# State-space layer: tokens to chunks and back as full 128x128 transposes of two groups or two token residues, copied out in strided pieces

## The reference

```
ug = u.reshape(bsz, L, 64, 16)
bu_re = einsum('blgh,gph->blgp', ug, bb_re)          # and bu_im
_, _, s_re, s_im = associative_scan(_ssm_combine, (a_re, a_im, bu_re, bu_im), axis=1)
y = einsum('blgp,ghp->blgh', s_re, c_re) - einsum('blgp,ghp->blgh', s_im, c_im)
y = gelu(y.reshape(bsz, L, 1024) + d_skip * u)
return y * sigmoid(y @ w_glu + b_glu)
```

## Time and profile before

| | us |
|---|---|
| median of 3 runs (lowest, highest) | 1896.31 (1896.26, 1896.64) |
| span of the profiled execution | 1895.6 |
| busy: PE, PEld, DVE | 1865.6, 1516.1, 1251.5 |
| busy: ACT, POOL | 904.5, 470.6 |

### The profile page before, as it was taken

One profiled execution on the slowest core, in us unless ns is written; L12 is line 12 of the kernel. 1 busy time (PEld: TensorE's weight loads), 2 busy tenths in 40 slices (PEclk: granted clock), 3 DMA queues, 4 the chain that ended last, 5 costly groups with the idle time before them and its releaser, 6 DMA issues.

```text
span 1895.6 us, 26223 instructions
## 1 busy us (share of the span) xinstructions
PE 1865.6 (98%) x10196; PEld 1516.1 (80%) x10196; DVE 1251.5 (66%) x1925; ACT 904.5 (48%) x1563; POOL 470.6 (25%) x506
## 2 busy tenths in 40 slices
PE   9999999999999999999999999999999999999998
PEld 7787877888667888968889887888787877688877
DVE  7998785647659436456457855678658467649364
ACT  5546877312288213542233344447545465545333
POOL 0491110574358514015123620020001300000000
PEclk9999999999999999999999999999999999999999
DMA  4226542335222535535626943521123411023221
GB/s 172 92 96 201 162 144 81 111 125 182 94 89 89 167 111 162 185 99 166 193 97 173 219 110 107 136 68 57 57 89 109 152 47 43 34 89 145 93 75 67
DMA packets 70874, 222.16 MB, mean 117 GB/s; under 512 B 17104, under 2 KB 17792, under 8 KB 69728
## 3 DMA queue, kind: packets, MB, share of 16 engines
q1 hardware_dynamic: 43056, 157.83, 25.1%
q0 software_dynamic: 24240, 55.79, 10.6%
q10 hardware_dynamic: 3456, 6.87, 1.3%
HBM read 203.23 MB, written 14.81 MB: 115 GB/s over the span
## 4 chain that ended last, share of the span: by engine, by line
PE 85%; DVE 9%; ACT 3%; issue 1%; DMA 1%; DVEq 0%; POOL 0%; SPq 0%; ACTq 0%
PE bank L489 24%; PE bank L491 23%; PE bank L490 23%; DVE ring_low L451 2%; PE bank L3706 1%; PE bank L2153 1%; PE bank L3739 1%; PE bank L1077 1%; PE bank L2160 1%; PE bank L2353 1%; PE bank L2326 1%; DVE lru_x L2254 1%; DVE sq L706 1%; PE bank L3478 1%; ACT ring_high L446 1%
## 5 line engine op out<-in xcount | busy, mean ns | idle before, releaser
L451 DVE TENSOR_TENSOR ring_low<-ring,ring_high 128x1024 fp32r<-128x1024 f32 x283 | 391.1, 1393 | 260.4 <-ACT ring_high L446 259.9
L446 ACT ACTIVATE ring_high<-ring 128x1024 fp32r<-128x1024 f32 x283 | 297.0, 1056 | 518.9 <-PE bank L491 518.4
L489 PE MATMUL bank<-h_high,ring_high 128*128 128x512 f32 (+1 forms) x1276 | 502.3, 394 | 8.1 <-DVE ring_low L451 6.1
L491 PE MATMUL bank<-h_high,ring_low 128*128 128x512 f32 (+1 forms) x1276 | 490.2, 384 | 0.0
L490 PE MATMUL bank<-h_low,ring_high 128*128 128x512 f32 (+1 forms) x1276 | 489.8, 384 | 0.0
L489 PEld LDWEIGHTS bank<-h_high,ring_high 128*128 128x128 f32 x1276 | 240.2, 188 | 71.6 <-issue 19.2
L490 PEld LDWEIGHTS bank<-h_low,ring_high 128*128 128x128 f32 x1276 | 240.3, 188 | 48.5 <-issue 3.1
L491 PEld LDWEIGHTS bank<-h_high,ring_low 128*128 128x128 f32 x1276 | 240.1, 188 | 48.0
L489 PE MATMUL bank<-gated_high,ring_high 128*128 128x512 f32 (+1 forms) x240 | 85.4, 356 | 1.1 <-DVE gated_low L3308 1.1
L491 PE MATMUL bank<-gated_high,ring_low 128*128 128x512 f32 (+1 forms) x240 | 83.2, 347 | 0.0
L490 PE MATMUL bank<-gated_low,ring_high 128*128 128x512 f32 (+1 forms) x240 | 83.2, 347 | 0.0
(11 more groups left out here) (573 smaller groups left out, 3748.3 us busy)
## 6 DMA issues: line engine op xcount, KB each, us to landing
ring<-slabs SPq DMA_DIRECT2D x289, 512.0 KB, 3.2
acs_rows<-acs_rows POOLq DMA_DIRECT2D x16, 512.0 KB, 4.7
s_outputs<-s_ca POOLq DMA_DIRECT2D x4, 1152.0 KB, 5.0
x<-xT SPq DMA_DIRECT2D x2, 2048.0 KB, 8.6
exp_acs<-acs_rows POOLq DMA_DIRECT2D x16, 256.0 KB, 10.3
s_b<-s_br POOLq DMA_DIRECT2D x8, 512.0 KB, 4.5
s_rows<-s_powers POOLq DMA_DIRECT2D x16, 256.0 KB, 7.4
s_inputs<-s_w POOLq DMA_DIRECT2D x8, 512.0 KB, 3.1
```

The lines of the kernel that those rows point to most:

```text
L446: act.activation(self.ring_high[:, self.splits_before[s] % AHEAD, :], self.ring[:, s % RING, :], ACT.Copy)\
L451: dve.tensor_tensor(self.ring_low[:, s % RING, :], self.ring[:, s % RING, :], self.ring_high[:, self.splits_before[s] % AHEAD, :].bitcast( ...
L489: pe.matmul(out, w[0], x[0], start=start, stop=False, **flags)
L491: return pe.matmul(out, w[1], x[0], start=False, stop=stop, **flags)
```

## The change

`transpose_in` now takes two groups at once: the 128x128 block of `u_tok` for groups 2q and 2q+1 is the weight, the whole identity is the moving operand, and the call is `pe.transpose`. A bank then holds, for each q, group parity on the partition halves and even and odd tokens in alternate columns. ACT sorts this out with four copies per bank in place of one: 64 partitions, 4 by 64 elements, read from PSUM with a step of two elements, written in runs of 64. `transpose_out` takes two token residues at once in the same way; the bank holds the residue's parity on the partition halves and the channel half in the column, and ACT again makes four copies of 64 partitions by 4 by 64 elements, this time with contiguous reads and with writes that step by 8 tokens.

```diff
@@ transpose_in
-                for g in range(8):
-                    w = L.UT[:, 8 * i + g].rearrange("p t h -> p (t h)")
-                    for e in range(2):
-                        t = pe.matmul(C.bank[u.b][half(1 - e), g * NC:g * NC + NC], w, C.ident[:, e:P:2], start=True, stop=True)
+                for q in range(4):
+                    two = L.UT[:, 8 * i + 2 * q:8 * i + 2 * q + 2].rearrange("p g t h -> p (g t h)")
+                    t = pe.transpose(C.bank[u.b][:, q * P:(q + 1) * P], two, C.ident[:])
                 t.then_inc(C.bank_full[u.b], 1)
@@ transpose_out
-                for r in range(8):
-                    for x in range(2):
-                        t = pe.matmul(C.bank[u.b][half(x), r * NC:r * NC + NC], L.YT[b % 2][:, r].rearrange("p k o -> p (k o)"),
-                                      C.ident[:, half(x)], start=True, stop=True)
+                for q in range(4):
+                    two = L.YT[b % 2][:, 2 * q:2 * q + 2].rearrange("p r k o -> p (r k o)")
+                    t = pe.transpose(C.bank[u.b][:, q * P:(q + 1) * P], two, C.ident[:])
                 t.then_inc(C.bank_full[u.b], 1)
@@ evac_u
-                act.activation(L.U[:, 8 * i:8 * i + 8, :].rearrange("p g c -> p (g c)"), C.bank[u.b][:], ACT.Copy)\
-                    .then_inc(C.bank_read[u.b], 1)
+                for n in range(2):
+                    got = C.bank[u.b][half(n), :].rearrange("p (q c e) -> p e q c", q=4, e=2)
+                    for e in range(2):
+                        ins = act.activation(L.U[half(1 - e), 8 * i + n:8 * i + 8:2, :], got[:, e], ACT.Copy)
+                ins.then_inc(C.bank_read[u.b], 1)
@@ back, on ACT
-                    act.activation(y.rearrange("p (c r) -> p r c", r=8), C.bank[u.b][:].rearrange("p (r c) -> p r c", r=8),
-                                   ACT.Copy).then_inc(y_made.sem, 1)
+                    for n in range(2):
+                        got = C.bank[u.b][half(n), :].rearrange("p (q x c) -> p x q c", q=4, x=2)
+                        for x in range(2):
+                            ins = act.activation(L.Y[half(x), i, :].rearrange("p (c q n) -> p n q c", q=4, n=2)[:, n], got[:, x], ACT.Copy)
+                    ins.then_inc(y_made.sem, 1)
```

## The result

The changed kernel takes 1903.67 us (median of 6 runs, 1901.22 to 1906.79), the kernel before 1896.85 us in the same session (6 runs, 1896.26 to 1897.69). The ratio is 1.0035, 95% interval 1.0025 to 1.0045: slower by 6.8 us, where +0.1 was forecast, and above the stated range of 1893.0 to 1900.8. The profiled execution has a span of 1901.9 us and a time of 1903.6. Two later sessions gave 1903.02 and 1903.21 for the same kernel, 1.0030 and 1.0029 of the kernel before.

A forecast was written before the change was run, and what follows sets the result against it. PE, busy 98% of the span, was taken as the bound, with ACT and its late loads just behind; -0.5 - 1.0 - 0.5 + 1.0 + 1.1 = +0.1 us gave 1896.4 us, forecast range 1895.0 to 1897.6, overall range 1893.0 to 1900.8.

The forecast's parts named there:

- rival 2: TensorE's clock drops in the new gaps of the stage: +1.6 to +3.2 us, 1898.0 to 1899.6; chance 0.16.
- The step that failed: ACT's neighbouring copies: each pair overlaps by 0.12 us, so four copies in take 1.15 us per bank, four out 2.2.
- The bounds: Alternatives around the sum: loads landing with PE 1893.9, cheaper copy-outs 1891.3, copies overlapping under 0.12 us 1897.2 or so.
- Start: Stage start, tr1 to z1: PE's 2.9 us saving mostly becomes waits for ACT's copies; z1 0.5 us early.
- tr6 and tr7: The two transposed banks behind z1, with banks long free: the full saving arrives, -1.0 us.
- PE per bank back: TensorE's transposes per bank on the way back: 0.93 us becomes 0.44; back0 gives -0.5 us in the sum.
- Middle: v4 to v7: loads of s_wv issued behind longer copy-outs make PE wait, 2.25 us at v5; +1.0 us.
- End: Stage end: two longer copy-outs delay gelu_low; k = 7 of the next product waits 1.9 us; +1.1 us.
- Behind the end: After the stage: PE is again the bound, ACT has about a microsecond of room; no term in the sum.
- Rival 1: ACT's stepped PSUM reads cost double, a copy-in 2.2 us: z1 2.8 late, +3.2 us, 1899.5; chance 0.22.
- Rival 3: PE's saving passes as the load queue begins earlier: 2.5 to 7.8 us less, 1894 to 1888.6; chance 0.15.
- Rival 4: The four transposes take as long as the sixteen matmuls, 0.23 us each; given no share.

The follow-up runs named there:

- the kernel with the way back alone: Kernel before with only the new transposes and four copies on the way back, way in as before: 1900.95 us, ratio 1.0016.
- the kernel with wide copies: The change with two 128-partition copies in and one old copy back, halves unsorted, so part of the layer is left out: 1893.68 us, 0.9981.
- the hybrid: Kernel before with the new form only at tr6, tr7 and back0 to back4: 1896.87 us, 1.0000; with loads of s_wv issued early 1895.07, 0.9989.

## Why the prediction was wrong

The picture was right: PE leads by a hair, ACT is the engine behind it, and every gain on PE turns into a wait. One figure in it was wrong, and all the steps with ACT's copies took it over. Two more things stood at nothing in the sum and cost something: the clock, which was left to rival 2, and what lies ahead of the stage.

*The step that failed* is "neighbours overlap by 0.60 - 0.48 = 0.12 us", taken from instructions over the same 128 partitions and used for copies over 64 that write one half and then the other. Those do not overlap. The single durations were right: 0.378 for the forecast 0.377, 0.655 for 0.63. But a copy-in takes 1.57 us per bank, not 1.15 (pace 1.03), and a copy-out 2.7, not 2.2. The bounds named this case ("if they overlap less than 0.12 each") and priced it only in the copy-outs, at 1897.2; at the start it was worth more, since there four copies in a row feed PE.

- **Start.** Forecast z1 0.5 early; measured 2.3 late (3.2 and 2.2 in the other two profiles). Up to tr1 all is as forecast: from L1758 it is 26.9 us before and after. Then tr2 was to come at 28.4 and came at 28.95, tr3 at 29.5 and came at 30.5, the fourth copy was to be over at 31.5 and was at 33.6. Those 2.1 us are the pace of the copies; z1 is 2.8 behind its forecast, and most of the remaining 0.7 goes with the clock of 0.58. The limit that I gave, z1 after 1036, was passed.
- **tr6 and tr7.** Forecast -1.0; from z1 to v2 it is 6.56 us for 7.63, -1.07 in each profile. Right.
- **PE per bank back.** Forecast 0.93 to 0.44. From the transposes to the next v it is 0.58 us, and a gap of 0.1 stands ahead of them: v2 to v4 gained 0.2, not 0.5. With it goes half of what the eight banks back should have given; the end keeps 0.65 from y7 to k0, for two banks.
- **Middle.** Forecast +1.0, through loads behind longer copies. In the kernel with the way back alone, where v4 is at least not late (0.3 early, forecast 2.0), it is +1.3 (v5 waits 2.94, forecast 2.25). In the change v4 is 1.05 late instead of 2.0 early, so the loads have that much more time: v5 waits 0.77, 0 and 1.44 us in the three profiles, and v4 to v7 gives back 0.9, 1.65 and 0.15. The mechanism was right and its size depends on what comes before. With the loads issued early, these waits are gone and the median is about 2 us lower in two pairs of kernels, by intervals that overlap.
- **End.** Forecast +1.1 at k7 relative to y7 and a wait of 1.9; measured +2.25 and 2.42. Two copy-outs of 2.7 for two of 1.13 are 3.1 us longer; less the 0.8 by which `gelu_low` had been early that is 2.3. The forecast had 2.2 for the copies and credited 0.35 for an earlier back6, which did not arrive.
- **Behind the end.** Forecast nothing, and in rival 2 a drop of clock. k7 to k14 takes 6.5 us for 4.8 in the first profile, with the clock at 0.79 over 8 us, and 4.9 at a clock of 1.00 in the second and third: 1.7 us in some executions.

By the steps of the first profile: +2.3 - 1.1 - 0.2 - 0.9 + 2.3 + 1.8 = +4.2 within the stage, of 4.3 measured. Against the forecast that is 2.8 more at the start, 0.3 more for back0, 1.9 less in the middle, 1.2 more at the end and 1.8 behind it. Of the 2.8 and the 1.2, the pace of the copies has 2.2 and 1.2; the clock has the rest of the start and the 1.8. The remaining 2.0 of the profile's 6.3 us lie ahead of it, where L1758 is late. In part that is chance of one execution, as the other profiles of the change have it 1.0 and 1.5 later than 1002.0. But the five profiles of kernels with all of the new single or doubled transposes and all four copies (three of the change, one with doubled transposes, one with early loads) have it at 1002.8 to 1004.0, and nine others at 1002.0 to 1002.4, one of which, with transposes as matmuls, has ACT's whole new work. In the changed kernel the shift is made in large part near 762 us, where PE waits 0.61 us for `ring_low` in another stage that the edit does not touch:

```profile
764.18 0.35 PE L489 MATMUL bank<-mem_high,ring_high 128*128 128x256 f32 x1 [0.61 <-DVE ring_low L451]
```

From L2160 (507 us) to L2326 (804 us) the three profiles of the change are 1.4, 0.6 and 0.9 us longer than the kernel before, and the one with doubled transposes 0.6. The one with early loads is not longer there; its 0.7 us are made before 312 us. What moves it is open; no experiment here was made for it. It is 1 to 2 us of the 6.

*The rivals.* Rival 1 (stepped PSUM reads double) is refuted: 375 to 382 ns each, and 0.66 us for two in the kernel with wide copies. It foresaw 1899.5, with the upper end of rival 2 (1899.6) the nearest of the forecasts, and for the start about the right size (z1 2.8 late), by a wrong cause: the copies are slow by not overlapping, not by their step. (Its pace of 1.9 should be 4 x (0.63 - 0.12) = 2.04 us by its own prices, which moves its z1 back by 0.4.) The Trainium skill, SBUF - State Buffer, in its note on cachelines has lines of 8 bytes for PSUM; for reads by ACT no price shows in these rows. Rival 2 (the clock) holds in part: about 0.5 to 1.6 us at the start, 1.7 at the end in some executions. Rival 3 (PE's saving passes) is seen only where ACT does not sort halves (1893.68). Rival 4: the transposes do take 0.11 us each.

Two readings of the prediction don't hold. The earlier trace rows end at 1106 us and so say nothing of the wait of 0.88 before y7; the windows of that trace behind 1107 do show 1.00. And "ACT is not later than before" contradicts the prediction's own end, by which the last low part is 0.85 later. It cost nothing that is seen: where the clock held, k7 to k14 took 4.9 us for 4.8.

The chance for slower by more than 0.2% was 0.16, as it took "rivals 1 and 2 together, or copies beyond double". No overlap instead of 0.12 us was within what the trace left open. Worked out as the sum was, it moves the fourth copy 2.1 us back at the start and `gelu_low` 1.2 at the end: up to +3.4 in all, 1899.7, with the clock's 0.7 and 1.7 on top of it near 1902.

## What to carry to other kernels

When one instruction becomes four, the price of a run of them is the pace at which the row advances, not the duration of one. Take that pace from a group in which the partitions change from one instruction to the next as they will in the new code, or leave it open. An order of the four copies by the half that they write was not tried here. Before PE is made faster in a stage, look who feeds it and for how long: here 7 of 16 banks had room, and those together with loads issued ahead of the longer copies made the only complete kernel that gained. A load that another engine issues behind a piece of work should be moved ahead of it before that piece grows; in the hybrid this also took most of the scatter out of the runs (1.1 us for 5.9).

## What the runs showed of the hardware

- ACT's neighbouring copies out of PSUM, 256 elements each: over the same 128 partitions a row advances by 0.26 to 0.28 us; over the same 64 partitions two take 0.64 us, so they overlap by 0.1; where a copy is on the other half from the one ahead of it, or only writes there, two take 0.76 and nothing overlaps. What a change of the reading half alone does was not measured. The Trainium skill, ScalarE: Activation LUTs, What ACT_TABLE_LOAD costs, gives an overlap of about 93 ns for instructions back to back; the copies on the same partitions agree, those that change the half do not.
- ACT reads every second fp32 of PSUM (step of 8 bytes) at the price of a contiguous read: 378 against 377 ns for 256 elements (386 over 128 partitions). Writes to SBUF with a step of 32 bytes cost 655 ns for 256.
- The granted clock fell at the start of the stage in all five profiles with single transposes between the waits for four copies, and held with the same transposes done twice: doing them keeps the clock as work does. Behind the single wait of 2.4 us at k7 it was 0.79 over 8 us in four profiles and 1.00 in three, so one execution does not tell whether such a gap costs clock.
- The same 512 KB load took from 4.8 to 10.5 us to land in this stage, at a DMA share of 0.95 to 1.06.
